# The order of half slabs and x turns where one sublayer of a two-layer float32 decoder trunk hands over to the next

## Chip, cores and metric

One of the eight cores of a Trainium2 chip runs the whole program. The metric is the device time of one execution in microseconds (us).

## The reference, cut to what matters

```
for layer in range(DEPTH):                      # DEPTH = 2
    h = rmsnorm(x, g_mix_pre[layer])
    y = even_mixer(...) or odd_mixer(...)       # q/k/v projection, attention, output projection
    x = x + rmsnorm(y, g_mix_post[layer])
    h = rmsnorm(x, g_mem_pre[layer])
    y = memory_cross_attention(h, memn, ...)
    x = x + rmsnorm(y, g_mem_post[layer])
    h = rmsnorm(x, g_ffn_pre[layer])
    y = conv_ffn(h, w_up, conv_w, conv_b, w_down)
    x = x + rmsnorm(y, g_ffn_post[layer])
```

`x` is 256 tokens by 2048 columns, float32. There are six sublayers (mix, mem, ffn in each of two layers), so there are five handovers from one sublayer's last projection to the next one's first. Each goes through two norms: `x` gets the normed `y` of the old sublayer, and the next projection takes `x` times a gain, column by column on the contraction axis (the factor of the next norm is applied to the product, later).

## The kernel before

A weight matrix streams through in slabs of 256 rows by 512 columns. A slab takes one of four slots (`RING`): its transfer fills `raw`, ScalarE (ACT) makes the rounded `w_hi` of it, and VectorE (DVE) the remainder `w_lo = raw - w_hi`. TensorE (PE) computes with three products per tile: a_hi·w_hi, a_hi·w_lo and a_lo·w_hi. The 256 tokens are two halves of 128, h = 0 and h = 1; `half_slab(h, ...)` is the six 128x512 matmuls of one slab for one half (2 tiles by 3 products, L1785, L1786, L1787).

The activations `a_hi`, `a_lo` of the next sublayer need `x` with columns on partitions, so `norm_turn(sub, i)` (L1844 in the profile) transposes two 128x128 tiles of `x_sb` per half on PE into a PSUM bank of `tp` or `aux`. The turns are numbered as items: items 0, 1 and 2 are the first three column pairs of half 0, items 3, 4 and 5 the same pairs of half 1, and items from 6 on take both halves (four transposes). An item goes through four engines: DVE adds the normed y (`norm_add`, x_new, L1084), PE turns it, ACT makes a_hi (`norm_hi`, L544), DVE makes a_lo (`norm_lo`, L1109). In `half_slab(..., ready)` a tile's matmuls wait for that tile's a_lo.

Every engine runs its own list in program order, written by hand; semaphores join the lists. What matters here:

- PE, `tail`: the last four slabs (k = 0 to 3, `TAIL`) of the old sublayer, first for half 0, then for half 1. Turns 0, 1 and 2 of the next sublayer (`after`) stand among the half slabs of half 1. `e` is the number of the first slab of the next sublayer.
- PE, `start`: half 0 of slabs 0, 1 and 2 (`LEAD`), then half 1 of the same slabs, with turns between; then whole slabs. Turns 3 and up need half 1 of x_new.
- ACT, `tail` and `start`: square(y 3,0), w_hi(e), a_hi item 0, w_hi(e+1), a_hi item 1, w_hi(e+2), square(y 3,1), a_hi item 2, w_hi(e+3), a_hi items 3 to 6. The square of the last y chunk (L554) gives the sum for half 1's norm factor.
- POOL (GpSimd), `y_rstd`: two small operations (L1733, L1735) from that sum to the factor of half 1; x_new of half 1 waits for it.
- DVE: x_new 0 to 2, w_lo(e), a_lo 0, w_lo(e+1), a_lo 1, w_lo(e+2), a_lo 2, x_new 3, x_new 4, y times gain, a_lo 3, x_new 5, a_lo 4, x_new 6, a_lo 5, w_lo(e+3), x_new 7, and so on. Behind an ffn, `y_add(sub, 3, 1, e)` (L1128) stands behind w_lo(e+2): the old y is the sum of two banks, and the square on ACT waits for it. In mem, one more square and gain of chunk (2, 1) stand ahead of item 0.

Of the kernel before, what the change touches and what calls it, by code (L numbers as in the profile page):

```python
# [50 lines left out]
RING = 4  # L51
AHEAD = 2
TAIL = 4
LEAD = 3
# [57 lines left out]
def build(nc, x, mem, positions, w_in_ab, w_out_ab, w_in_c, b_f, w_out_c,  # L112
# [6 lines left out]
    with ctx:  # L119
# [158 lines left out]
        def LV(layer, name, value):  # L278

            return sem(name), value + layer * PER_LAYER.get(name, 0)  # L280
# [49 lines left out]
        SUBS = []  # L330
# [9 lines left out]
        def S(sub, name):  # L340
            return sem(f"{sub[0]}_{name}")

        def SV(sub, name, value):


            before = 0 if sub[0] == "mix" and name in ("x_new", "xT", "a_hi", "a_lo") else PER_LAYER.get(name, 0)
            return sem(f"{sub[0]}_{name}"), value + sub[1] * before
# [40 lines left out]
        def y_cols(h, g):  # L388

            return yg[:, h, g * N:(g + 1) * N]  # L390
# [676 lines left out]
        def _(dve):  # L1067
            def split(n, s):


                dve.wait_ge(hi_ready, n + 1)
                dve.tensor_tensor(w_lo[:, s], raw[:, s], w_hi[:, s].bitcast(F32), ALU.subtract).then_inc(lo_ready, 1)  # L1072

            def ahead(n, s=None):
                if isinstance(n, int) and n + AHEAD >= TOTAL_SLABS:
                    return
                split(n + AHEAD, (n + AHEAD) % RING if s is None else (s + AHEAD) % RING)
# [9 lines left out]
            def norm_add(sub, i):  # L1087

                s, hs = item(sub, i)
                if prev_sub(sub):  # L1090
                    for h in hs:
                        add_y(prev_sub(sub), h, s * SLAB_KT * P, SLAB_KT * P, S(sub, "x_new"))
# [11 lines left out]
            def norm_lo(sub, i):  # L1104

                dve.wait_ge(*SV(sub, "a_hi", SLAB_KT * (i + 1)))
                for j in range(SLAB_KT):
                    bank, kt, cols = item_tile(sub, i, j)
                    dve.scalar_tensor_tensor(out=a_lo[:, kt, cols], in0=bank, scalar=gain(sub, kt),  # L1109
                                             in1=a_hi[:, kt, cols].bitcast(F32),  # L1110
                                             op0=ALU.mult, op1=ALU.subtract).then_inc(S(sub, "a_lo"), 1)

            def y_gain(sub, g, h):


                dve.wait_ge(*SV(sub, f"g_landed_{g % 2}", 16 * (g // 2 + 1)))
                dve.wait_ge(*SV(sub, "y_sq", y_count(sub, g, h)))
                y = y_cols(h, g) if sub[0] == "ffn" else acc[:, g % 2, h, :]
                dve.tensor_tensor(y_cols(h, g), y, g_post[:, g % 2, :], ALU.mult).then_inc(S(sub, "yg_done"), 1)

            def y_add(sub, g, h, n_done):

                if n_done is None:
                    dve.wait_ge(*SV(sub, "y_half", TAIL))
                else:
                    dve.wait_ge(slab_used, n_done)
                dve.wait_ge(*LV(sub[1], "u_out", 4 * (g // 2 + 1)))
                dve.tensor_tensor(y_cols(h, g), acc[:, g % 2, h, :], y_cols(h, g), ALU.add).then_inc(S(sub, "y_acc"), 1)  # L1128
# [63 lines left out]
            def tail(sub, after, e):  # L1192

                ahead(e - 4)
                if sub[0] == "mem":
                    for h in range(HALF):
                        y_gain(sub, 1, h)
                ahead(e - 3)
                if sub[0] == "ffn":
                    y_add(sub, 3, 0, None)  # L1200
                if sub[0] == "mem":
                    y_gain(sub, 2, 0)
                y_gain(sub, 3, 0)
                for i in range(LEAD):
                    norm_add(after, i)
                ahead(e - 2)
                if sub[0] == "mem":
                    y_gain(sub, 2, 1)
                norm_lo(after, 0)
                ahead(e - 1)  # L1210
                norm_lo(after, 1)
                split(e + 2, (e + 2) % RING)
                if sub[0] == "ffn":
                    y_add(sub, 3, 1, e)


            dve.memset(a_lo[:, KT - 1, :].bitcast(F32), 0.0).then_inc(zeros_set, 1)
# [469 lines left out]
            e = TOTAL_SLABS  # L1687
# [82 lines left out]
        def _(pe):  # L1770
# [64 lines left out]
            def norm_turn(sub, i):  # L1835

                s, hs = item(sub, i)
                pe.wait_ge(*SV(sub, "x_new", added(sub, i)))
                if i >= 4:
                    pe.wait_ge(*SV(sub, "a_lo", SLAB_KT * (i - 3)))  # L1840
                for j in range(SLAB_KT):
                    to, kt, _ = item_tile(sub, i, j)
                    for k, h in enumerate(hs):
                        last = pe.transpose(to[:, k * P:(k + 1) * P], x_sb[:, h, kt * P:(kt + 1) * P], ident[:])  # L1844
                last.then_inc(S(sub, "xT"), 1)
# [5 lines left out]
            def start(sub, n):  # L1851

                if sub == SUBS[0]:
                    for j in range(SLAB_KT):
                        pe.wait_ge(*((first_w[1], hi_ready)[j], 1))
                        pe.wait_ge(first_a[0], j + 1)
                        for h in range(HALF):
                            pe.matmul(acc[:, 0, h, :], a_hi[:, j, h * P:(h + 1) * P], w_hi[:, 0, j, :],
                                      start=(j == 0), stop=False)
                        pe.wait_ge(*((first_w[2], lo_ready)[j], 1))  # L1860
                        for h in range(HALF):
                            pe.matmul(acc[:, 0, h, :], a_hi[:, j, h * P:(h + 1) * P], w_lo[:, 0, j, :],
                                      start=False, stop=False)
                        pe.wait_ge(first_a[1], j + 1)
                        for h in range(HALF):
                            last = pe.matmul(acc[:, 0, h, :], a_lo[:, j, h * P:(h + 1) * P], w_hi[:, 0, j, :],
                                             start=False, stop=False)
                    last.then_inc(slab_used, 1)
                    for s in range(1, GS):
                        pe.wait_ge(lo_ready, n + s + 1)  # L1870
                        for h in range(HALF):
                            for j in range(SLAB_KT):
                                last = tile_products(h, (n + s) % RING, 0, j, SLAB_KT * s + j, KT, a_hi, a_lo,
                                                     (first_a[1], SLAB_KT * s + j + 1) if h == 0 else None)
                        last.then_inc(slab_used, 1)
                    return
                for s in range(LEAD if sub != SUBS[0] else 0):
                    pe.wait_ge(lo_ready, n + s + 1)
                    half_slab(0, (n + s) % RING, 0, SLAB_KT * s, KT, a_hi, a_lo, a_ready(sub, s))
                    if s >= 1:  # L1880
                        norm_turn(sub, LEAD + s - 1)
                for s in range(LEAD if sub != SUBS[0] else 0):
                    half_slab(1, (n + s) % RING, 0, SLAB_KT * s, KT, a_hi, a_lo, a_ready(sub, LEAD + s))\
                        .then_inc(slab_used, 1)
                    norm_turn(sub, 2 * LEAD - 1 + s)
                for s in range(LEAD, GS):
                    slab(n + s, (n + s) % RING, 0, SLAB_KT * s, KT, a_hi, a_lo, a_ready(sub, LEAD + s))
                    if LEAD + s + 2 < ITEMS:
                        norm_turn(sub, LEAD + s + 2)

            def tail(sub, after, e, kts, hi, lo):


                per = kts // SLAB_KT
                for h in range(HALF):
                    for k in range(TAIL):
                        at = D_GROUPS * per - TAIL + k
                        g, s = at // per, at % per
                        if h == 0:
                            if s == 0:  # L1900
                                y_free(sub, g)
                            pe.wait_ge(lo_ready, e - TAIL + k + 1)
                        last = half_slab(h, (e - TAIL + k) % RING, g % 2, SLAB_KT * s, kts, hi, lo)
                        last.then_inc(slab_used if h else S(sub, "y_half"), 1)
                        if h and k and after:
                            norm_turn(after, k - 1)

            def y_free(sub, g):

# [11 lines left out]
            for L in range(LAYERS):  # L1921
# [233 lines left out]
                for g in range(2):  # L2155
                    for s in range(MEM_GS):
                        k = g * MEM_GS + s
# [174 lines left out]
```

## Time and profile before

| | |
|---|---|
| time, median of 3 runs | 2457.3 us (2455.97 to 2457.34) |
| the profiled execution | 2456.99 us, its span 2454.9 us |
| busy of the span | PE 2436.8, DVE 1691.1, ACT 1318.8, POOL 55.6 us |
| weight transfers | 468.33 MB, mean 191 GB/s |
| granted clock of PE | 0.999 over the span |

Where a row says "idle before", it is the time in which an engine had nothing running just before that instruction, and the arrow names what ended it. A matmul's duration is modelled and overlaps the next one, so distances between PE starts say more than durations. Of two or more instructions that a row merges, the start is that of the first.

### The profile page before, as it was taken

The page shows a single profiled execution, that of the slowest core. Times are in us where ns is not written, and L with a number is a line of the kernel's source. Part 1 is how long each engine was busy: PE and PEld are TensorE (multiplying, and loading weights), DVE is VectorE, ACT ScalarE, POOL GpSimd, SP SyncE. Part 2 cuts the span into 40 slices and gives each one's busy share as a digit, 9 for nine tenths or more (in the row PEclk, how much of TensorE's full clock was granted, in tenths as well). Part 3 has the DMA queues.
Part 4 walks back from the last instruction along what each step waited for, and adds up shares of the span by engine and source line. Part 5 has one row for each costly group of instructions (what it writes and reads, how often), then busy time and mean ns, then how long its engine had stood idle before and what let it go on. Part 6 is the DMA issues. An engine that isn't in the chain of part 4 may idle for free.

```text
span 2454.9 us, 34925 instructions
## 1 busy us (share of the span) xinstructions
PE 2436.8 (99%) x12460; PEld 2077.0 (85%) x12460; DVE 1691.1 (69%) x2366; ACT 1318.8 (54%) x1897; POOL 55.6 (2%) x119
## 2 busy tenths in 40 slices
PE   9999999999999999999999999999999999999998
PEld 7888888888888888888888888888888888888887
DVE  6555666677777677778665466566777776778786
ACT  6345555665555555555454455556655555555553
POOL 0000000000000000000000002000000000000000
PEclk9999999999999999999999999999999999999999
DMA  8657455556656655656566675555566565656664
GB/s 288 195 185 250 148 165 172 185 165 196 186 183 192 193 181 187 218 193 215 182 192 183 200 213 168 171 176 172 180 187 199 174 194 188 193 181 208 203 215 155
DMA packets 247022, 468.33 MB, mean 191 GB/s; under 512 B 17520, under 2 KB 20736, under 8 KB 246912
## 3 DMA queue, kind: packets, MB, share of 16 engines
q1 hardware_dynamic: 234640, 447.83, 57.6%
q10 hardware_dynamic: 12272, 19.04, 2.4%
q8 instruction: 69, 1.13, 0.2%
q14 instruction: 41, 0.34, 0.0%
HBM read 464.69 MB, written 2.11 MB: 190 GB/s over the span
## 4 chain that ended last, share of the span: by engine, by line
PE 96%; DVE 2%; ACT 1%; DMA 0%; issue 0%; POOL 0%; DVEq 0%; SPq 0%; POOLq 0%; ACTq 0%
PE acc L1806 15%; PE acc L1785 10%; PE acc L1787 10%; PE acc L1786 10%; PE aux L1806 8%; PE acc L1814 8%; PE tp L1806 7%; PE acc L2211 5%; PE acc L2210 5%; PE acc L2209 5%; PE aux L1814 4%; PE tp L1814 4%; DVE w_lo L1072 1%; PE tp L2026 1%; PE acc L2047 1%
## 5 line engine op out<-in xcount | busy, mean ns | idle before, releaser
L1072 DVE TENSOR_TENSOR w_lo<-raw,w_hi 128x1024 fp32r<-128x1024 f32 x847 | 1020.6, 1222 | 548.0 <-ACT w_hi L501 544.5
L501 ACT ACTIVATE w_hi<-raw 128x1024 fp32r<-128x1024 f32 x847 | 868.5, 1055 | 386.3 <-PE acc L1787 127.6
L1806 PE MATMUL acc<-a_hl,w_hi 128*128 128x512 f32 x1568 | 486.4, 391 | 0.0
L1785 PE MATMUL acc<-w_hi,a_hl 128*128 128x512 f32 x988 | 391.4, 396 | 1.7 <-DVE a_hl L1100 1.6
L1787 PE MATMUL acc<-w_hi,a_hl 128*128 128x512 f32 x988 | 385.5, 390 | 0.0
L1786 PE MATMUL acc<-w_lo,a_hl 128*128 128x512 f32 x988 | 384.8, 389 | 0.0
L1806 PEld LDWEIGHTS acc<-a_hl,w_hi 128*128 128x128 f32 x1568 | 282.0, 189 | 47.3
L1814 PE MATMUL acc<-a_hl,w_lo 128*128 128x256 f32 x1568 | 315.0, 283 | 0.0
L1814 PEld LDWEIGHTS acc<-a_hl,w_lo 128*128 128x128 f32 x1568 | 257.0, 191 | 15.3
L1806 PE MATMUL aux<-a_hl,w_hi 128*128 128x512 f32 x832 | 256.9, 390 | 0.0
L1806 PE MATMUL tp<-a_hl,w_hi 128*128 128x512 f32 x736 | 227.3, 390 | 0.0
L1785 PEld LDWEIGHTS acc<-w_hi,a_hl 128*128 128x128 f32 x988 | 185.6, 188 | 39.8 <-DVE w_lo L1072 2.0
L1787 PEld LDWEIGHTS acc<-w_hi,a_hl 128*128 128x128 f32 x988 | 185.4, 188 | 39.4
L1786 PEld LDWEIGHTS acc<-w_lo,a_hl 128*128 128x128 f32 x988 | 185.8, 188 | 36.3
L2209 PE MATMUL acc<-w_hi,hid_hi 128*128 128x512 f32 x512 | 199.2, 389 | 0.0
L2210 PE MATMUL acc<-w_lo,hid_hi 128*128 128x512 f32 x512 | 199.2, 389 | 0.0
L2211 PE MATMUL acc<-w_hi,hid_lo 128*128 128x512 f32 x512 | 199.2, 389 | 0.0
L1806 PEld LDWEIGHTS aux<-a_hl,w_hi 128*128 128x128 f32 x832 | 156.2, 188 | 34.1
L1814 PE MATMUL aux<-a_hl,w_lo 128*128 128x256 f32 x832 | 167.6, 283 | 0.0
L1806 PEld LDWEIGHTS tp<-a_hl,w_hi 128*128 128x128 f32 x736 | 138.2, 188 | 30.1
L1814 PE MATMUL tp<-a_hl,w_lo 128*128 128x256 f32 x736 | 148.3, 283 | 0.0
L1814 PEld LDWEIGHTS aux<-a_hl,w_lo 128*128 128x128 f32 x832 | 129.4, 191 | 0.0
(263 smaller groups left out, 2506.7 us busy)
## 6 DMA issues: line engine op xcount, KB each, us to landing
raw<-in_w_up SPq DMA_DIRECT2D x352, 512.0 KB, 4.1
raw<-in_w_down SPq DMA_DIRECT2D x176, 512.0 KB, 4.7
raw<-in_w_in_c SPq DMA_DIRECT2D x96, 512.0 KB, 4.3
raw<-in_w_in_ab SPq DMA_DIRECT2D x95, 512.0 KB, 4.5
raw<-in_w_out_ab SPq DMA_DIRECT2D x32, 512.0 KB, 4.5
raw<-in_w_out_c SPq DMA_DIRECT2D x32, 512.0 KB, 4.3
raw<-in_w_mk SPq DMA_DIRECT2D x16, 512.0 KB, 4.1
raw<-in_w_mq SPq DMA_DIRECT2D x16, 512.0 KB, 4.2
```

Of the source, the lines that this page charges most:

```text
L501: act.activation(w_hi[:, s], raw[:, s], ACT.Copy).then_inc(hi_ready, 1)
L1072: dve.tensor_tensor(w_lo[:, s], raw[:, s], w_hi[:, s].bitcast(F32), ALU.subtract).then_inc(lo_ready, 1)
L1785: pe.matmul(o, hi[:, kt, rows], w_hi[:, slot, j, :], start=(kt == 0), stop=False)
L1786: pe.matmul(o, hi[:, kt, rows], w_lo[:, slot, j, :], start=False, stop=False)
L1787: return pe.matmul(o, lo[:, kt, rows], w_hi[:, slot, j, :], start=False, stop=(kt == kts - 1))
L1806: last = pe.matmul(bank, w_hi[:, slot, j, f * P:(f + 1) * P], both, start=(kt == 0), stop=(kt == KT - 1))
L1814: last = pe.matmul(bank[:, SEQ:2 * SEQ], w_lo[:, slot, j, f * P:(f + 1) * P], a_hi[:, kt, :], start=False, stop=False)
L2026: last = pe.matmul(o, qkT[:, q, t * P:(t + 1) * P], qkT[:, k, 0:b - a], start=True, stop=True)
L2047: pe.matmul(o, v_sb[:, 0, cols], probT[:, h % 2, 0:SEQ], start=True, stop=False)
L2209: pe.matmul(o, a_h, b_h, start=first, stop=False)
L2210: pe.matmul(o, a_h, b_l, start=False, stop=False)
L2211: return pe.matmul(o, a_l, b_h, start=False, stop=last)
```

## The change

Three edits. In `start`, half 0 of slabs 0, 1 and 2 stand in a row, and turns 3 and 4 stand together behind them, ahead of half 1 of slab 0 (before, turn 3 stood behind half 0 of slab 1, and turn 4 behind half 0 of slab 2). In `tail`, turns 0 and 1 stand together behind half 1 of k = 2, and turn 2 stays behind k = 3 (before, turn 0 stood behind k = 1). On DVE, in the tail of an ffn, `y_add(sub, 3, 1, e)` stands ahead of `split(e + 2)`, which makes w_lo(e+2).

```diff
@@ DVE, tail @@
                 norm_lo(after, 1)
-                split(e + 2, (e + 2) % RING)
                 if sub[0] == "ffn":
                     y_add(sub, 3, 1, e)
+                split(e + 2, (e + 2) % RING)
@@ PE, start @@
                     half_slab(0, (n + s) % RING, 0, SLAB_KT * s, KT, a_hi, a_lo, a_ready(sub, s))
-                    if s >= 1:
-                        norm_turn(sub, LEAD + s - 1)
+                if sub != SUBS[0]:
+                    norm_turn(sub, LEAD)
+                    norm_turn(sub, LEAD + 1)
@@ PE, tail @@
                         last.then_inc(slab_used if h else S(sub, "y_half"), 1)
-                        if h and k and after:
-                            norm_turn(after, k - 1)
+                        if h and after and k == TAIL - 2:
+                            norm_turn(after, 0)
+                            norm_turn(after, 1)
+                        if h and after and k == TAIL - 1:
+                            norm_turn(after, 2)
```

PE, beginning of the mem sublayer of layer 0, before: behind half 0 of slab 1 comes turn 3 (aux), then half 0 of slab 2, then turn 4 (tp).

```order
L1787 MATMUL acc<-w_hi,a_hl 128x512
L1844 MATMUL aux<-ident,x_sb 128x128 x2
L1785 MATMUL acc<-w_hi,a_hl 128x512
L1786 MATMUL acc<-w_lo,a_hl 128x512
L1787 MATMUL acc<-w_hi,a_hl 128x512
L1785 MATMUL acc<-w_hi,a_hl 128x512
L1786 MATMUL acc<-w_lo,a_hl 128x512
L1787 MATMUL acc<-w_hi,a_hl 128x512
L1844 MATMUL tp<-ident,x_sb 128x128 x2
```

The same place of the change: half 0 of slab 2, both turns, and half 1 of slab 0 at once behind them.

```order
L1785 MATMUL acc<-w_hi,a_hl 128x512
L1786 MATMUL acc<-w_lo,a_hl 128x512
L1787 MATMUL acc<-w_hi,a_hl 128x512
L1785 MATMUL acc<-w_hi,a_hl 128x512
L1786 MATMUL acc<-w_lo,a_hl 128x512
L1787 MATMUL acc<-w_hi,a_hl 128x512
L1844 MATMUL aux<-ident,x_sb 128x128 x2
L1844 MATMUL tp<-ident,x_sb 128x128 x2
L1785 MATMUL acc<-w_hi,a_hl 128x512
```

Turn 3 has moved behind six matmuls, and between turn 3 and half 1 of slab 0 there is now only turn 4. In the tail turn 0 moves behind six matmuls in the same way.

DVE, handover from the ffn of layer 0 to the mix of layer 1, as a difference: the rows are a_lo 1, w_lo(e+2), y_add, a_lo 2 and x_new 3 and 4.

```order
 L1072 TENSOR_TENSOR w_lo<-raw,w_hi 128x1024
 L1109 SCALAR_TENSOR_TENSOR a_hl<-aux,gT,a_hl 128x128 x2
-L1072 TENSOR_TENSOR w_lo<-raw,w_hi 128x1024
 L1128 TENSOR_TENSOR yg<-acc,yg 128x512
+L1072 TENSOR_TENSOR w_lo<-raw,w_hi 128x1024
 L1109 SCALAR_TENSOR_TENSOR a_hl<-tp,gT,a_hl 128x128 x2
 L1084 SCALAR_TENSOR_TENSOR x_sb<-yg,stats,x_sb 128x256 x2
```

One subtraction has moved behind y_add; nothing else on DVE, ACT, POOL or the transfer queue changes its place.

## Rows read from the trace of the kernel before

**Rows 1.** The page, part 1: busy us, share of the span, count.

```profile
PE 2436.8 (99%) x12460; PEld 2077.0 (85%) x12460; DVE 1691.1 (69%) x2366; ACT 1318.8 (54%) x1897; POOL 55.6 (2%) x119
```

**Rows 2.** Line L1844, the turns: idle of PE and PEld before it, times.

```profile
  DVE x_sb L1084: 12.1, 17
```

**Rows 3.** Timeline, PE, mix to mem, layer 0: start, duration, what.

```profile
410.44 0.39 PE L1785 MATMUL acc<-w_hi,a_hl 128*128 128x512 f32 x1
...
411.81 0.38 PE L1844 MATMUL tp<-ident,x_sb 128*128 128x128 f32 x2
...
418.02 0.39 PE L1844 MATMUL aux<-ident,x_sb 128*128 128x128 f32 x2
...
419.79 0.48 PE L1785 MATMUL acc<-w_hi,a_hl 128*128 128x512 f32 x1
...
422.86 0.60 PE L1844 MATMUL tp<-ident,x_sb 128*128 128x128 f32 x4
```

**Rows 4.** Timeline, ACT, same handover.

```profile
412.23 0.62 ACT L544 ACTIVATE a_hl<-tp,gT 128x128 fp32r<-128x128 f32 x2 [0.47 <-PE tp L1844]
412.74 1.06 ACT L501 ACTIVATE w_hi<-raw 128x1024 fp32r<-128x1024 f32 x1
...
414.35 1.06 ACT L501 ACTIVATE w_hi<-raw 128x1024 fp32r<-128x1024 f32 x1
415.30 0.60 ACT L554 ACTIVATE junk<-acc 128x512 f32<-128x512 f32 x1
...
415.86 0.63 ACT L544 ACTIVATE a_hl<-tp,gT 128x128 fp32r<-128x128 f32 x2
...
418.45 0.63 ACT L544 ACTIVATE a_hl<-aux,gT 128x128 fp32r<-128x128 f32 x2 [1.00 <-PE aux L1844]
```

**Rows 5.** Timeline, DVE, same handover.

```profile
413.83 1.23 DVE L1072 TENSOR_TENSOR w_lo<-raw,w_hi 128x1024 fp32r<-128x1024 f32 x1
414.97 0.60 DVE L1109 SCALAR_TENSOR_TENSOR a_hl<-aux,gT,a_hl 128x128 fp32r<-128x128 f32 x2
415.49 1.22 DVE L1072 TENSOR_TENSOR w_lo<-raw,w_hi 128x1024 fp32r<-128x1024 f32 x1
416.62 0.60 DVE L1109 SCALAR_TENSOR_TENSOR a_hl<-tp,gT,a_hl 128x128 fp32r<-128x128 f32 x2
417.43 0.88 DVE L1084 SCALAR_TENSOR_TENSOR x_sb<-yg,stats,x_sb 128x256 f32<-128x256 f32 x2 [0.20 <-POOL stats L1735]
...
419.11 0.61 DVE L1109 SCALAR_TENSOR_TENSOR a_hl<-aux,gT,a_hl 128x128 fp32r<-128x128 f32 x2 [0.20 <-ACT a_hl L544]
```

**Rows 6.** Groups by form, 408 to 436 us: count, busy, mean ns.

```profile
L1109 DVE SCALAR_TENSOR_TENSOR a_hl<-aux,gT,a_hl 128x128 fp32r<-128x128 f32 x6 | 1.8, 345 | 0.4 <-ACT a_hl L544 0.4
```

**Rows 7.** Timeline, PE: turns that waited, handovers mem-ffn, ffn-mix, mem-ffn.

```profile
498.40 0.44 PE L1844 MATMUL aux<-ident,x_sb 128*128 128x128 f32 x2 [0.37 <-DVE x_sb L1084]
...
1221.32 0.44 PE L1844 MATMUL tp<-ident,x_sb 128*128 128x128 f32 x2 [0.82 <-DVE x_sb L1084]
...
1229.46 0.44 PE L1844 MATMUL aux<-ident,x_sb 128*128 128x128 f32 x2 [1.71 <-DVE x_sb L1084]
...
1715.14 0.44 PE L1844 MATMUL tp<-ident,x_sb 128*128 128x128 f32 x2 [0.33 <-DVE x_sb L1084]
...
1721.90 0.44 PE L1844 MATMUL aux<-ident,x_sb 128*128 128x128 f32 x2 [0.33 <-DVE x_sb L1084]
```

**Rows 8.** Timeline, DVE, then ACT, ffn to mix.

```profile
1226.41 0.69 DVE L1128 TENSOR_TENSOR yg<-acc,yg 128x512 f32<-128x512 f32 x1
...
1228.93 0.87 DVE L1084 SCALAR_TENSOR_TENSOR x_sb<-yg,stats,x_sb 128x256 f32<-128x256 f32 x2
...
1227.14 0.63 ACT L554 ACTIVATE junk<-yg 128x512 f32<-128x512 f32 x1 [2.15 <-DVE yg L1128]
```

**Rows 9.** Timeline, POOL: the power of the norm factor, two handovers.

```profile
410.38 0.57 POOL L1735 TENSOR_TENSOR stats<-stats,minus_half 128x1 f32<-128x1 f32 x1
...
1719.79 1.53 POOL L1735 TENSOR_TENSOR stats<-stats,minus_half 128x1 f32<-128x1 f32 x1
```

## The prediction

> **What bounds the kernel now.** I read the page first: PE is busy 99% of the span, the other engines far less [rows 1]. So PE sets the end, and the order of its work costs nothing but the waits in it. Then I read who waits at the turns: PE and its weight loads sat idle 12.1 us before L1844, 17 times, always until an x_new of DVE [rows 2]. That counts both queues of PE, so it is an upper bound and no sum of lost time. The lost time is read from PE's timeline at the five handovers. Call them T1 (mix to mem, 411 us), T2 (mem to ffn, 492), T3 (ffn to mix, 1221), T4 (mix to mem, 1635), T5 (mem to ffn, 1715).
>
> Lengths on PE first. Half 1 of k = 1 starts at 410.44 and turn 0 at 411.81, so six matmuls take 1.37, 0.23 each [rows 3]. From turn 3 (418.02) to half 1 of slab 0 (419.79) there are turn, half slab, turn: 1.77. With a turn of two transposes at 0.14, the half slab behind a turn takes 1.48. Four transposes last 0.60 where two last 0.38, so a pair of turns holds PE for 0.14 + 0.22 = 0.36. The "idle" of rows 7 counts from the modelled end of a matmul (0.39 long); counted from where the next could have started, each wait is 0.16 longer: turn 3 of T2 waits 0.53, turns 0 and 3 of T3 wait 0.98 and 1.87, turns 0 and 3 of T5 wait 0.49 and 0.49 [rows 7]. Turns 0 and 3 in T1 and T4 don't wait at all: there the idle is missing in the row, and the distances are those of the matmuls [rows 3]. A turn that has waited takes 0.06 more (0.44 against 0.38). So 4.4 us, with 0.3 for the restarts, is all that the moved turns can give back. At all five handovers turn 7 waits as well, behind DVE's list; nothing here changes the order of that list ahead of it.
>
> **What the change does, step by step, in T1.** The question is what the turns' customers get. After a turn's start, ACT's a_hi follows 0.42 later (411.81 to 412.23) and holds ACT 0.51; w_hi holds it 0.95; the square 0.56 [rows 3, 4]. a_lo starts 0.66 after a_hi (418.45 to 419.11); a_lo holds DVE 0.52 and w_lo 1.13 [rows 4, 5]. w_lo starts 1.09 after w_hi (412.74, 413.83). PE can start on the first tile of a_lo when that is written: 0.35 [rows 6], and 0.05 to 0.08 more, as from x_new (1228.93, 0.48 long) to the turn at 1229.46 [rows 7, 8]. I take 0.42. So from a turn to the half slab that uses it there are 0.42 + 0.66 + 0.42 = 1.50 us. Before, turn 3 had 1.77 to its customer: covered, by half 0 of slab 2. Now it has 0.36.
>
> New T1, forward. Half 1 of k = 2 starts at 411.81, the pair of turns at 413.18, k = 3 at 413.54, turn 2 at 415.02, half 0 of slab 0 at 415.16. ACT: a_hi 0 at 413.60 (before 412.23), w_hi(e+1) 414.11, a_hi 1 415.06, w_hi(e+2) 415.57, square 416.52 (before 415.30), a_hi 2 417.08. DVE: w_lo(e+1) 415.20, a_lo 1 416.34, w_lo(e+2) 416.86, a_lo 2 418.00. PE: half 0 of slab 1 could start at 416.64 and starts with a_lo 1 at 416.76; half 0 of slab 2 could start at 418.13 and starts with a_lo 2 at 418.42; turns 3 and 4 at 419.79; a_hi 3 420.21, a_lo 3 420.87; half 1 of slab 0 at 421.29. Before it was 419.79: **1.50 us later**. 0.41 of it is the queue on ACT and DVE that turn 0, moved late, pushes back; 1.14 is the wait behind the pair (1.50 less 0.36); 0.05 is rounding and the missing turn. Queued behind the waiting matmul are all later matmuls of PE, nothing else can fill it. From there turn 5, a_hi 5, a_lo 5, w_lo(e+3), x_new 7 and turn 7 keep their distances, as their chain begins at turn 5. So the 1.50 stays.
>
> The new x_new 3: before, it started 2.13 behind the square (415.30 to 417.43). In T1 that gives 418.65, the turn could go at 419.18, and PE comes at 419.79. It has 0.61 to spare.
>
> Here a rule bears. POOL's power takes 0.57 in one handover and 1.53 in T5 [rows 9]; in T5 it lies beside a w_lo subtraction (DVE's list has w_lo(e+2) there). The Trainium skill, SBUF — State Buffer, section "SBUF: two separate sides", says that GpSimd and a DVE operation with two SBUF inputs take a shared port pair as an exclusive lock, so that the later one waits for the whole instruction. By that rule w_lo(e+2), now running from 416.86 to 418.08 with the square's end inside it, holds POOL's first step until 418.1 and x_new 3 starts near 418.7; the turn would still not wait, and the sum is the same. Were POOL to take the pair first, w_lo(e+2) would come up to 0.57 later; that is the second rival below.
>
> **T4** has T1's lists and rows: +1.50. **T2** has T1's lists and a square and gain more ahead of item 0, which lie in the time before the later turn. Its turn 3 waited 0.53 and 0.06 restart, which the new order covers, since PE comes later anyway: 1.50 − 0.59 = +0.91. **T5** waited so twice, 0.55 each: 1.50 − 1.10 = +0.40. **T3** has the DVE edit as well. Half 1 of k = 2 starts at 1220.34 (turn 0 at 1221.32 less 0.98), the pair at 1221.71, k = 3 at 1222.07, half 0 of slab 0 at 1223.69. a_hi 0 1222.13, w_hi(e+1) 1222.64, a_hi 1 1223.59; w_lo(e+1) 1223.73, a_lo 1 1224.86, y_add 1225.38 (before 1226.41), w_lo(e+2) 1225.98; the square 0.73 behind y_add [rows 8] at 1226.11 (before 1227.14), a_hi 2 1226.68, a_lo 2 1227.34; half 0 of slab 2 at 1227.76, turns 3 and 4 at 1229.13 (x_new 3 at 1226.11 + 2.13 = 1228.24, so no wait), half 1 of slab 0 at 1230.63, before 1229.46 + 1.81 = 1231.27: **−0.64**. Without the edit on DVE, T3 would lose 0.5: y_add stood 1.13 later.
>
> **The sum**: 1.50 + 0.91 − 0.64 + 1.50 + 0.40 = 3.7 us. To this comes a restart of 0.06 for a matmul that has waited, once per handover at least, 0.3: **+4.0 us**. Two turns side by side save one change between transposes and matmuls: apart 2 x 0.25, together 0.47, so 0.03, ten times, 0.3 at most; I leave it out of the sum and in the range. The profiled execution took 2456.99, 0.3 below the median of 2457.3; with the sum it would be 2461.0, and the median 2461.3. I say 2461.2. Slabs arrive early enough: w_lo(e+1) and w_lo(e+2) are some 1.4 later, and the transfers that reuse those slots with them, but the next w_hi that needs them stands behind a_hi 6.
>
> **The bounds.** No row shows a half slab waiting for a_lo. Below, 0.35 (a_lo written, no delay) instead of 0.42 takes 0.07 from each of three waits in a row, 0.2 per handover: 1.0, so +2.7 with the saved changes. Above, a waiting half slab could pay the 0.06 at three places instead of one and 0.1 more at each for its weight load (0.19 long, otherwise hidden): up to 0.42 per handover more than counted: 2.1, so +6.1.
>
> **Rivals.**
> 1. *Waits for waits.* The saved waits are real (4.4 us in rows 7) and the new ones smaller than worked out, so nothing is left: 0 to +2.5, 2457 to 2459.8. For it: my 0.41 from the ACT and DVE queues rests on every gap being closed. Against: 1.14 is plain arithmetic from turn to a_lo.
> 2. *Slower by more than 0.2%.* The norm factor of half 1 comes so late that turns 3 and 4 wait for x_new, in T1, T2, T4 and T5. It decides if square to x_new 3 takes over 2.74 us (419.79 − 0.53 − 416.52), where rows show 2.13 and, with the stretched power, about 2.7. At 3.2 it is 0.5 each, 2.0 in all; or POOL's lock pushes w_lo(e+2) by 0.57: 2.3. With the sum: 2463.2 to 2463.6. The upper bound above (2463.4) is in the same place.
> 3. *Faster.* The wait at half 1 of slab 0 doesn't arise, because a_hi 3 and a_lo 3 are ready by the end of turn 4. Then 1.14 falls away five times, and the sum is 3.7 − 5.7 = −2.0, 2455.2; with the saved changes and no queue delay −4 at best. For it there is only that turns 0 and 3 of T3 waited most, and T3 is where DVE's order is mended.
> 4. *Nothing changes*, because turns are hidden anyway: excluded for T3, likely for none.
>
> **Chances.** The measurement can tell about 0.2%, 4.9 us. The forecast (+2.5 to +5.5) 0.65; rival 1 0.12; rival 2 0.17; rival 3 0.06. Of the forecast 0.12 lie beyond 4.9. So slower 0.29, same 0.64, and faster 0.07 with the best case of rival 3 and what I have overlooked. The range 2457.9 to 2464.0 leaves out most of rival 3 and part of rivals 1 and 2, two in ten.
>
> **What would show it.** In the new profile: half 1 of slab 0 starts 1.5 us behind turn 3 at all five handovers, with "idle before" on PE or its weight load, ended by a_lo (L1109), some 1.1 us each; turns 0 and 3 with no idle; turn 7 still late; the square of T1 some 1.2 us later behind w_hi(e+2); in T3 y_add directly behind a_lo 1. It is wrong if half 1 of slab 0 follows turn 4 without a gap, if turns 3 still wait for x_new, or if turn 7 comes without its wait and gives time back.

## The result: 0.18% slower

| | before | changed |
|---|---|---|
| time, median of 20 runs each | 2456.91 us | 2461.05 us |
| ratio, 95% interval | | 1.0018 [1.0012, 1.0024] |
| the profiled execution, its span | 2456.99, 2454.9 us | 2461.56, 2459.8 us |

One of the changed kernel's 20 runs was slow (2686.57 us, granted clock 0.85) and counts in nothing but the median. The difference of the medians is 4.1 us.

The page of the changed kernel, part 1, then the clock of part 2 (answers to [rows 1]):

```profile
PE 2439.5 (99%) x12460; PEld 2077.1 (84%) x12460; DVE 1691.2 (69%) x2366; ACT 1318.4 (54%) x1897; POOL 56.3 (2%) x119
...
PEclk9999999999999999999999999999999999999999
```

The instruction counts are the same, only PE's waits differ. Line L1844's idle (answers to [rows 2]):

```profile
  DVE x_sb L1084: 2.5, 5
```

And the waits of PE's weight loads, of the whole span: who waited for whom, us in total, times, longest.

```profile
PEld acc L1785 <- DVE w_lo L1072: 8.3, 13, 2.0
PEld acc L1785 <- DVE a_hl L1109: 5.6, 5, 1.1
PEld aux L1844 <- DVE x_sb L1084: 2.5, 5, 0.5
```

The turns' 12.1 us of idle have become 2.5, all of it turn 7. In their place half slabs wait: five times for a_lo (half 1 of slab 0, 1.1 us each), and 13 times behind a w_lo, 8.3 us in all, where the kernel before had 3 such waits with 3.0 us. The ten new ones are half 0 of slabs 1 and 2 at each of the five handovers. The change did remove the waits that it aimed at, and made others. Timeline of PE in T1, turns, half slabs 1 and 2 of half 0, half 1 of slab 0 (answers to [rows 3]):

```profile
411.46 0.39 PE L1785 MATMUL acc<-w_hi,a_hl 128*128 128x512 f32 x1
...
412.82 0.38 PE L1844 MATMUL tp<-ident,x_sb 128*128 128x128 f32 x2
...
414.80 0.48 PE L1785 MATMUL acc<-w_hi,a_hl 128*128 128x512 f32 x1
...
416.49 0.47 PE L1785 MATMUL acc<-w_hi,a_hl 128*128 128x512 f32 x1
...
418.14 0.47 PE L1785 MATMUL acc<-w_hi,a_hl 128*128 128x512 f32 x1
...
419.60 0.38 PE L1844 MATMUL aux<-ident,x_sb 128*128 128x128 f32 x2
419.82 0.38 PE L1844 MATMUL tp<-ident,x_sb 128*128 128x128 f32 x2
421.08 0.50 PE L1785 MATMUL acc<-w_hi,a_hl 128*128 128x512 f32 x1 [0.89 <-DVE a_hl L1109]
```

From turn 3 (419.60) to its customer, the half slab that uses it (421.08), there are 1.48 us. The pair of turns takes 0.36 of that, the rest is the wait. What it waited for, on ACT and then on DVE (answers to [rows 4, 5]): item 3's a_hi and a_lo, and ahead of them the queue that the later turn 0 pushed back.

```profile
413.25 0.63 ACT L544 ACTIVATE a_hl<-tp,gT 128x128 fp32r<-128x128 f32 x2 [1.83 <-PE tp L1844]
...
416.16 0.61 ACT L554 ACTIVATE junk<-acc 128x512 f32<-128x512 f32 x1
...
420.02 0.63 ACT L544 ACTIVATE a_hl<-aux,gT 128x128 fp32r<-128x128 f32 x2 [1.70 <-PE aux L1844]
```

```profile
416.00 0.60 DVE L1109 SCALAR_TENSOR_TENSOR a_hl<-aux,gT,a_hl 128x128 fp32r<-128x128 f32 x2
416.51 1.22 DVE L1072 TENSOR_TENSOR w_lo<-raw,w_hi 128x1024 fp32r<-128x1024 f32 x1
417.65 0.60 DVE L1109 SCALAR_TENSOR_TENSOR a_hl<-tp,gT,a_hl 128x128 fp32r<-128x128 f32 x2
418.45 0.88 DVE L1084 SCALAR_TENSOR_TENSOR x_sb<-yg,stats,x_sb 128x256 f32<-128x256 f32 x2 [0.20 <-POOL stats L1735]
...
420.68 0.61 DVE L1109 SCALAR_TENSOR_TENSOR a_hl<-aux,gT,a_hl 128x128 fp32r<-128x128 f32 x2 [0.75 <-ACT a_hl L544]
```

### How a handover is measured from here on

A change of 1 us in one place can't be told from times that spread over 4 us, but it can from PE's starts. I take the length of a handover from the first matmul of half 1 of k = 1 to the first matmul of slab 3, in every profile. In before, T1 is 410.44 to 425.41, 14.97. Both ends are the same matmuls in every kernel here.

| kernel | T1 | T2 | T3 | T4 | T5 | sum | span |
|---|---|---|---|---|---|---|---|
| before | 14.97 | 15.52 | 17.92 | 14.96 | 16.05 | 79.4 | 2454.9 |
| changed | 16.66 | 17.07 | 17.48 | 16.66 | 17.02 | 84.9 | 2459.8 |
| changed, second execution | 16.66 | 16.86 | 17.48 | 16.63 | 16.65 | 84.3 | 2459.1 |
| start edit alone | 16.06 | 17.23 | 18.50 | 16.08 | 16.60 | 84.5 | 2459.7 |
| tail edit alone | 16.33 | 16.72 | 19.58 | 16.31 | 16.33 | 85.3 | 2460.1 |
| DVE edit alone | 14.96 | 15.99 | 16.82 | 14.94 | 15.80 | 78.5 | 2454.0 |
| start and tail | 16.67 | 17.91 | 20.88 | 16.61 | 16.65 | 88.7 | 2463.4 |
| tail and DVE | 16.33 | 17.20 | 16.90 | 16.33 | 16.31 | 83.1 | 2458.7 |
| before, gain row's buffer | 14.95 | 15.53 | 17.90 | 14.95 | 15.53 | 78.9 | 2453.1 |
| changed, gain row's buffer | 16.63 | 16.61 | 17.48 | 16.62 | 16.62 | 84.0 | 2459.7 |
| before, x_new 6 and 7 earlier | 14.59 | 15.49 | 17.56 | 14.60 | 15.42 | 77.7 | 2452.0 |
| three edits, PE's order of before | 14.60 | 15.17 | 16.43 | 14.60 | 15.18 | 76.0 | 2451.3 |

Each row is one profiled execution. What an edit doesn't touch comes back: T1 and T4 have before's order in three of these kernels (before, DVE edit alone, before with the gain row's buffer) and take 14.94 to 14.97 in all. T2 and T5 don't come back so well; why is shown below.

Between the two profiled executions the handovers differ by +1.69, +1.55, −0.44, +1.70 and +0.97, together +5.5; the way to T1 was 0.3 shorter in the changed one (410.10 against 410.44), and some 0.3 went elsewhere. That makes the 4.9 of the spans.

### The profile page after: what moved, and what is told of

Read it like the earlier page. It is cut to its first block, busy times and chain, and to the rows that moved or that the text cites. A ratio compares the mean times of both kernels' runs of the same rounds, so it can differ in the third digit from the quotient of the medians.

```text
span 2459.8 us, 34925 instructions
## 1 busy us (share of the span) xinstructions
PE 2439.5 (99%) x12460; PEld 2077.1 (84%) x12460; DVE 1691.2 (69%) x2366; ACT 1318.4 (54%) x1897; POOL 56.3 (2%) x119
## 4 chain that ended last, share of the span: by engine, by line
PE 95%; DVE 2%; ACT 1%; DMA 1%; issue 0%; POOL 0%; DVEq 0%; SPq 0%; POOLq 0%; ACTq 0%
PE acc L1806 15%; PE acc L1785 10%; PE acc L1787 10%; PE acc L1786 10%; PE aux L1806 8%; PE acc L1814 8%; PE tp L1806 7%; PE acc L2213 5%; PE acc L2214 5%; PE acc L2215 5%; PE aux L1814 4%; PE tp L1814 4%; PE tp L2030 1%; DVE w_lo L1072 1%; PE acc L2051 1%
```

## The experiments

### Each edit by itself

The start edit: the two lines of the diff under "PE, start", nothing else.

```diff
-                    if s >= 1:
-                        norm_turn(sub, LEAD + s - 1)
+                if sub != SUBS[0]:
+                    norm_turn(sub, LEAD)
+                    norm_turn(sub, LEAD + 1)
```

> Only the edit in start (turns 3 and 4 behind the three half slabs of half 0); tail and DVE as before. A handover's length is counted from half 1 of k=1 to the first matmul of slab 3; in the profile of before the five are 14.97, 15.52, 17.92, 14.96, 16.05 us. Theory A (a wait of 1.1 us behind the pair of turns, since turn to a_lo takes 1.50): T1 and T4 +1.2 each, T2 and T5 +0.6 each (the wait of turn 3 for x_new, 0.5, is covered), T3 +0.5 (turn 3 waited 1.87, covered for 1.4); in all +4.1 us. Rival (the late queue on ACT and DVE, from the tail, is the main loss, the pair's wait a small one): under +1.5 in all.

Measured: +1.09, +1.71, +0.58, +1.12, +0.55, in all +5.1 (one run, 2461.5 us beside 2455.8 of before on that chip). T1, T3, T4 and T5 are as theory A has them; T2 is 1.1 too long, and its turn 0, which this edit doesn't touch, stood 2.46 behind k = 1 instead of 1.36: the landing of a transfer, below. The rival falls: the wait behind the pair is there without any late queue.

The tail edit:

```diff
-                        if h and k and after:
-                            norm_turn(after, k - 1)
+                        if h and after and k == TAIL - 2:
+                            norm_turn(after, 0)
+                            norm_turn(after, 1)
+                        if h and after and k == TAIL - 1:
+                            norm_turn(after, 2)
```

> Only the edit in tail (turns 0 and 1 together behind k=2). Theory A (turn 0, 1.36 later, pushes w_hi, a_hi, the square and so x_new 3 back by about 1.2): turn 3 waits for x_new in T1 and T4, which it did not before; T1 and T4 +1.3 each, T2 +0.8, T3 +0.1 (turn 0's wait of 0.98 is covered), T5 +0.2 to +0.6; in all +3.7 to +4.1. So the two edits overlap: each alone costs about what both cost, since the late x_new is hidden by the late turn 3. Rival (each edit costs its own share of 1.69 in T1, 0.5 from the tail, 1.2 from start): T1 +0.5.

Measured: +1.36, +1.20, **+1.66**, +1.35, +0.28 (2461.9 us). T1 and T4: each edit alone costs 1.1 and 1.35, both together 1.69, not 2.5. So the two overlap, as expected: with turn 3 late, the late x_new is hidden. T2 is 0.4 above the +0.8 of theory A; its gain row was used 5.5 us behind its issue, before's 4.3 (see below). T3 was a miss, by 1.6. The timeline of PE in T3 for this kernel shows the reason: turn 3 waited 2.58, and soon behind it matmuls and turns take 0.63 that took 0.39.

```profile
1231.46 0.44 PE L1844 MATMUL aux<-ident,x_sb 128*128 128x128 f32 x2 [2.58 <-DVE x_sb L1084]
1231.65 0.48 PE L1785 MATMUL acc<-w_hi,a_hl 128*128 128x512 f32 x1
...
1232.81 0.63 PE L1786 MATMUL acc<-w_lo,a_hl 128*128 128x512 f32 x1
1233.24 0.63 PE L1787 MATMUL acc<-w_hi,a_hl 128*128 128x512 f32 x1
1233.67 0.63 PE L1844 MATMUL tp<-ident,x_sb 128*128 128x128 f32 x2
```

The same kernel in stretches of 2 us; the granted clock is the number behind POOL's. It fell to the lower of its two levels (0.50 in slices of half a microsecond, 1.2 GHz) and came back:

```profile
1230.00:1232.00 2.00, 0.54 (x4) 0.50 (x5) 1.59 (x5) 1.38 (x4) 0.74 (x2) 1.00 0.95 329
1232.00:1234.00 2.00, 2.00 (x9) 1.53 (x7) 1.41 (x4) 0.56 (x2) 0.00 (x0) 0.62 0.16 58
1234.00:1236.00 2.00, 2.00 (x7) 1.62 (x6) 1.01 (x4) 0.62 (x2) 0.00 (x0) 0.53 0.03 8
1236.00:1238.00 2.00, 2.00 (x12) 1.56 (x11) 1.00 (x4) 0.62 (x2) 0.00 (x0) 1.00 0.00 0
```

The DVE edit:

```diff
-                split(e + 2, (e + 2) % RING)
                 if sub[0] == "ffn":
                     y_add(sub, 3, 1, e)
+                split(e + 2, (e + 2) % RING)
```

> Only the edit on DVE (y_add ahead of w_lo(e+2) behind an ffn). Theory A: it bears on T3 alone, where the square, the norm factor, x_new 3 and turn 3 all come 1.1 earlier: T3 17.92 to 16.8, the others as before; the time 1.1 us less, under what the times can tell. Rival (w_lo(e+2), pushed back 0.6, makes half 0 of slab 2 wait, or POOL is held by it): T3 gains under 0.5.

Measured: T3 −1.10, T1 and T4 the same, T2 +0.47 and T5 −0.25 with the landing of the gain row (used 5.1 and 4.8 us behind its issue, before's 4.3 and 5.1). The time was 2455.8 us, the same as before's single run on that chip; a gain of 1.1 us is under what one run can tell. T3 is as expected.

### Two more on T3, for the clock

The change without its DVE edit, then the tail edit with the DVE edit. Both are made of the pieces shown above.

> The change without its edit on DVE: both PE edits, y_add behind w_lo(e+2) as before. Lengths of T1, T2, T4, T5 as in the change (16.7, 16.9 to 17.1, 16.7, 16.7 to 17.0). Theory A by order alone: T3 is 1.1 longer than the change's 17.48, so 18.6. Theory K (a PE wait of over 2 us in T3 lets the granted clock fall to 0.5, as with the tail edit alone, where a wait of 2.58 did): half 0 of slab 2 would wait 1.15 + 1.1 = 2.3 there; if that is long enough T3 comes at 19.5 to 20.5 with a granted clock under 0.7 in the 2 us behind the wait, if not at 18.6 with clock 1.00.

Measured: T3 20.88, so 3.40 longer than in the change (2465.2 us). Theory K, and 0.4 above the upper end that it gave, since the clock stayed low for 6.8 us, against 3.4 with the tail edit alone. T2 came at 17.91, 0.8 above its range, by the gain row (used 6.3 us behind its issue). The half slab that waits, and the stretches behind it:

```profile
1231.73 0.47 PE L1785 MATMUL acc<-w_hi,a_hl 128*128 128x512 f32 x1 [2.03 <-DVE a_hl L1109]
...
1234.00:1236.00 2.00, 1.32 (x5) 0.88 (x4) 0.95 (x4) 1.14 (x4) 0.00 (x0) 0.50 0.00 0
1236.00:1238.00 2.00, 2.00 (x6) 1.56 (x5) 1.36 (x5) 0.00 (x0) 0.00 (x0) 0.50 0.03 8
1238.00:1240.00 2.00, 2.00 (x8) 1.57 (x7) 0.49 (x2) 0.63 (x2) 0.00 (x0) 0.65 0.00 0
```

> Tail edit and DVE edit, start as before. With the tail edit alone T3 took 19.58 us, turn 3 waited 2.58 and the granted clock fell to 0.53 behind it. Theory K (1.3 to 1.4 of that T3 is the fallen clock): with y_add 1.1 earlier turn 3 waits 1.5, the clock stays at 1.00, and T3 is 16.9 to 17.2, so 2.4 to 2.7 less for an edit that gave 1.10 by itself. Rival (no clock effect, the order alone makes T3 long): 18.4 to 18.5. T1 and T4 as with the tail edit alone, 16.3.

Measured: T3 16.90, clock 1.00, and turn 3 with this row:

```profile
1231.63 0.44 PE L1844 MATMUL aux<-ident,x_sb 128*128 128x128 f32 x2 [1.47 <-DVE x_sb L1084]
```

So y_add's move is worth 1.10 by order [DVE edit alone], 2.68 on top of the tail edit and 3.40 within the change. The excess, 1.6 and 2.3 us, is there where the clock fell, and nowhere else. The starts on PE show the same split. The instruction that waited starts only 1.1 us later without y_add's move in both pairs (turn 3 at 10.58 behind k = 1 against 9.47; half 0 of slab 2 at 10.03 against 8.89); the rest comes behind it: from there to slab 3 it takes 9.00 against 7.43, and 10.85 against 8.59. In the change itself the clock held at T3: both waits there count 0.88 and 0.89, and its stretches from 1226 to 1236 all show 1.00.

### The gain row's landing, T2 and T5

The changed kernel again:

> The changed kernel once more. Its handovers were 16.66, 17.07, 17.48, 16.66, 17.02 us. If the lengths are set by order alone (theory A), all five come back within 0.1. If the landing of the gain row (g_post, 5.5 us behind its issue in T2, where the kernel before had 4.3) sets T2 and T5 (theory G), T2 and T5 move by up to 0.5 with the landing while T1, T3 and T4 come back.

Measured: T1, T3, T4 within 0.03; T2 −0.21, T5 −0.37 (2460.9 us). From issue to use the gain row took 5.27 us in T2 and 5.06 in T5, in the first execution 5.51 and 5.46: now 0.24 and 0.40 less. Theory G. DVE multiplies the last chunk of y by a gain row that arrives by transfer. Its rows on DVE, before and in the changed kernel, T2 each; the issue by ACT was at 485.94 and 487.31:

```profile
485.94 0.33 ACTq L573 DMA_DIRECT2D g_post<-in_g_mem_post  x1
...
490.23 0.69 DVE L1119 TENSOR_TENSOR yg<-acc,g_post 128x512 f32<-128x512 f32 x1 [2.31 <-DMA g_post<-in_g_mem_post]
```

```profile
487.31 0.34 ACTq L573 DMA_DIRECT2D g_post<-in_g_mem_post  x1
...
492.82 0.69 DVE L1119 TENSOR_TENSOR yg<-acc,g_post 128x512 f32<-128x512 f32 x1 [3.53 <-DMA g_post<-in_g_mem_post]
```

4.3 us from issue to use in the one and 5.5 in the other. To settle it, the row got a buffer of its own, which lets it be loaded early. In short, with comments added and DVE's waits for the new semaphore left out:

```diff
+        g_last = place("g_last", [P, N], at=big_at + 40 * KB)
...
-                    gain_chunk(sub, 3)                      # in tail, behind w_hi(e-1)
...
+                    if sub[0] == "mem" and g == 1 and s == 0:
+                        gain_chunk(sub, 3)                  # into g_last, with its own semaphore
```

On the kernel before:

> The kernel before, with one edit: the mem sublayer's last gain row (chunk 3) has a buffer of its own and its load is issued at the beginning of chunk 1, several us earlier. Theory G (the landing of that row, 4.3 to 5.7 us behind its issue, sets turn 0 in T2 and T5 and is what made them differ between executions): turn 0 stands 1.36 to 1.37 behind the start of k=1 in T2 and T5, both 15.5 long, no idle of DVE until a transfer of g_post. Rival (turn 0 is set by the norm factor from POOL or by ACT): T2 and T5 stay between 15.5 and 16.1 with turn 0 at 1.6 or later.

Measured: T2 and T5 15.53, turn 0 at 1.37 and 1.36 (2454.9 us beside a median of 2456.6). DVE now waits for ACT's square there, not for a transfer:

```profile
1711.63 0.69 DVE L1131 TENSOR_TENSOR yg<-acc,g_last 128x512 f32<-128x512 f32 x1 [2.01 <-ACT junk L555]
```

On the change:

> The change, with the gain row's own buffer and early load in mem. Theory G: T2 and T5, 17.07 and 17.02 in one execution of the change and 16.86 and 16.65 in another, both come to 16.65, the length of T1 and T4, since their turns come at the same places and their waits for x_new 3 are hidden; against 15.53 with the same buffer and the order of before, the change then costs 1.1 in each. Rival (something else of mem, its extra square and gain, makes T2 and T5 longer): 16.9 or more.

Measured: T2 16.61, T5 16.62 (2461.5 us). With this disturbance out of both, the change costs +1.68, +1.08, −0.42, +1.67 and +1.09, together +5.1 us.

### A version that beats both

x_new 6 and 7 ahead, in gaps in which DVE waited for a_hi:

```diff
                     norm_add(sub, 5)
+                    norm_add(sub, 6)
                     norm_lo(sub, 4)
-                    norm_add(sub, 6)
+                    norm_add(sub, 7)
                     norm_lo(sub, 5)
                     split(n + 3, (n + 3) % RING)
-                    norm_add(sub, 7)
                     norm_lo(sub, 6)
```

> The kernel before, with one edit on DVE: in start, x_new 6 stands ahead of a_lo 4 and x_new 7 ahead of a_lo 5, in DVE's idle gaps of 0.6 and 0.2, so that w_lo(e+3) no longer stands ahead of x_new 7. Theory A: turn 7 comes without its wait at all five handovers, 0.35 to 0.4 less each: 14.6, 15.1 plus what the gain row adds, 17.5, 14.6, 15.1 plus the same; 1.9 in all. Rival: x_new 6 ahead of a_lo 4 makes half 1 of slab 1 wait, and the gain is gone.

Measured: 14.59, 15.49, 17.56, 14.60, 15.42 (2454.1 us beside 2456.6). T1, T3 and T4 are 0.36 to 0.38 shorter. Turn 7 of T1 stands 0.23 behind the last matmul ahead of it, without idle:

```profile
423.58 0.39 PE L1787 MATMUL acc<-w_hi,a_hl 128*128 128x512 f32 x1
423.81 0.60 PE L1844 MATMUL aux<-ident,x_sb 128*128 128x128 f32 x4
```

All three on the order of before:

> The kernel before with three DVE and load edits together and PE's order untouched: y_add ahead of w_lo(e+2) behind an ffn, x_new 6 and 7 earlier, the gain row's own buffer. Theory A with G: 14.6, 15.1, 16.4, 14.6, 15.1, sum 75.8 against 79.4 before and 84.9 in the change: 3.0 to 3.6 us less than before, ratio 0.9986 to 0.9990. Rival (the waits saved come back elsewhere): the sum falls, the span doesn't.

Measured: 14.60, 15.17, 16.43, 14.60, 15.18, sum 76.0; 2452.8 us, median of 11 runs, against 2456.6 of before (median of 15), **ratio 0.9984 [0.9975, 0.9993]**. That is 3.8 us less, where 3.0 to 3.6 stood; the interval holds both. Page, part 1:

```profile
PE 2435.5 (99%) x12460; PEld 2078.3 (85%) x12460; DVE 1691.9 (69%) x2366; ACT 1319.2 (54%) x1897; POOL 55.2 (2%) x119
```

## Why the prediction was right, point by point

The time (2461.2 forecast, 2461.05 measured) and the mechanism held. The single terms were less exact than the total, and that the total fits to 0.15 us is luck.

- **A turn's customer comes 1.50 us behind it**: 1.48 in T1, and 1.48 to 1.49 at the other four. This was the main term, and the start edit alone shows it (+1.09 and +1.12 where 1.14 stood).
- **The queue on ACT and DVE, 0.41 in T1**: half 0 of slab 1 waited 0.22 (forecast 0.12), of slab 2 0.19 (0.29); together 0.41. (The prediction's parts, 0.41 and 1.14, make 1.55; its 0.05 comes off, to give 1.50.) The square came 1.20 later against PE's own clockwork (416.16 here, 415.30 − 0.34 before), as forecast.
- **T1 and T4, +1.50 each**: +1.69 and +1.70. What was short is the restart. I took 0.06 once per handover. In T1 half 0 of slab 2, which had waited, took 1.46 to turn 3 (418.14 to 419.60), where one in a stream takes 1.37; the one before it likewise, and half 1 of slab 0 took 1.53 to turn 5, where 1.47 had stood: 0.09 + 0.09 + 0.06. With 1.50 that is 1.74 against 1.69. It lay within the upper bound.
- **T3, −0.64**: −0.44 (−0.42 with the buffer), short by 0.2, as T1 is. Both halves of the reason are shown: the DVE edit alone gives −1.10, the PE edits take back 0.7 of it. What I did not see is what the DVE edit prevents. I said that T3 would lose 0.5 without it; it lost 2.96, and 2.3 of that is the fallen clock.
- **T2, +0.91**: +1.55, of which 0.5 is the gain row's landing in that execution; with it pinned +1.08.
- **T5, +0.40: here a step failed.** I subtracted turn 0's wait of 0.55 as covered, since PE comes to it later. It came back as a wait of half 0 of slab 0 (0.57 from turn 2 to it, where 0.14 is the rule), because everything between, DVE's x_new 0 to 2, w_lo(e), the additional gain of mem and a_lo 0, hangs on the same late gain row. The rows of T5 in the changed kernel, DVE from the late gain row to a_lo 0, then PE's turn 2 and half 0 of slab 0:

```profile
1718.30 0.69 DVE L1119 TENSOR_TENSOR yg<-acc,g_post 128x512 f32<-128x512 f32 x1 [3.48 <-DMA g_post<-in_g_mem_post]
...
1721.83 0.60 DVE L1109 SCALAR_TENSOR_TENSOR a_hl<-tp,gT,a_hl 128x128 fp32r<-128x128 f32 x2
```

```profile
1721.75 0.38 PE L1844 MATMUL tp<-ident,x_sb 128*128 128x128 f32 x2
1722.32 0.47 PE L1785 MATMUL acc<-w_hi,a_hl 128*128 128x512 f32 x1 [0.19 <-DVE a_hl L1109]
```

  A wait moved behind its cause is saved only if the chain behind the cause has slack. In the second execution, where the row landed earlier, T5 was +0.60 against before, and with the row pinned in both +1.09. I had named the idle of turn 0 without asking whether the row that ended it would be the same in another execution.
- **The sum** was 4.0 and the handovers gave 5.5 in the profiled pair, 5.1 with the transfer pinned; the medians differ by 4.1, and the interval of the ratio covers 2.9 to 5.9. The 5.1 is the forecast's 4.0 with two terms put right: restarts as in T1 made each handover 0.1 to 0.2 longer than forecast, the 0.06 for one restart counted in (0.6 in all), and turn 0's wait in T5 was not saved (0.5). That the medians differ by 4.1 and not by 5.1 is inside the interval and not explained.
- **Rival 2**, the norm factor too late for turn 3: not so in the change, where no turn 3 waits for x_new; but it is what the tail edit alone does (T1 turn 3 at 8.89 behind k = 1 where 7.58 was). **Rival 3** fell with the five rows of a_lo. **Rival 1**: the saved waits were real, the new ones larger, not smaller.
- **POOL's first step beside w_lo(e+2)**: in T1 of the changed kernel it took 0.19 at 409.77, with no w_lo beside it, and 0.78 at 417.00, beside w_lo(e+2) (416.51, 1.22 long), and ended with it. In T2 of the changed kernel, from the timelines of POOL and DVE:

```profile
498.57 1.22 POOL L1733 TENSOR_TENSOR stats<-stats 128x1 f32<-128x1 f32 x1 [4.21 <-ACT junk L554]
...
498.53 1.21 DVE L1072 TENSOR_TENSOR w_lo<-raw,w_hi 128x1024 fp32r<-128x1024 f32 x1
```

  So the trace agrees with the rule that the prediction names (the Trainium skill, SBUF — State Buffer, "SBUF: two separate sides": the later of the two waits for the whole instruction). The step costs nothing here, as forecast, since turn 3 came later still. Nor does it make T2 and T5 of the best version 0.57 longer than T1: POOL's step ends with w_lo(e+2) in both places, and it is w_lo(e+2) that stands 0.57 later, behind k = 1 at 5.06 in T1 and 5.63 in T2, with the additional gain of mem (0.60) ahead of it in DVE's list:

```profile
492.17 0.69 DVE L1131 TENSOR_TENSOR yg<-acc,g_post 128x512 f32<-128x512 f32 x1
...
494.94 1.22 DVE L1078 TENSOR_TENSOR w_lo<-raw,w_hi 128x1024 fp32r<-128x1024 f32 x1
```

  No experiment moved that gain, so this cause is read from the rows and not tested.

## What to carry to other kernels

Count the distance from a producer to its customer in an in-order engine's list before moving anything between them: a half slab between turn and use was the cover of a 1.5 us chain through two other engines, and putting the producers side by side removed it. A wait on the critical engine is gone only if the chain behind its cause is shorter too; look for what feeds the late value (here a gain row in a shared buffer, and one addition queued behind a subtraction) and mend that. Where a time can't resolve an edit, the start-to-start length of the stretch in one profile can, as long as no transfer lands in it: T2 and T5 moved by 0.2 and 0.4 us between two executions of one kernel.

## What was not expected of the hardware

- The granted clock fell to 0.50 to 0.53 after PE had been idle 2.58 us in T3 with the tail edit alone and 2.03 us with both PE edits; it did not after 1.71 in before, 1.47 with the tail and DVE edits, or two waits of 0.88 and 0.89 in the change. In both cases PE ran at full pace for 0.8 to 1.0 us first, and in both it had waited some 0.2 us earlier, as it had with the tail and DVE edits, where the clock held. It cost 1.6 and 2.3 us, about as much as the waits. Each case is one execution.
- A 256 KB row spread to 128 partitions, issued by ACT beside the weight stream, was used 4.3 to 5.7 us behind its issue in 16 of the 18 handovers T2 and T5 that had it, with nothing changed ahead of it, 6.2 in T2 of the tail and DVE edits and 6.3 in T2 of the start and tail edits (issue 486.56, use 492.90). That moved a handover by up to 1.3 us (T2 17.91 there, 16.61 with the row pinned).
- A half slab of half 0 that resumes after a wait takes 1.46 to 1.47 us where it took 1.37 to 1.38 in a stream, so about 0.1 us beyond the wait. Half 1 of slab 0, which stood behind a turn and took 1.47 to 1.48 before, takes 1.48 to 1.53.
